# Opening of a two-block kernel: square sums on TensorE, the last shift piece in halves, the step unit two tiles ahead of the x unit, most constants loaded behind the weights

## The reference, cut to what matters

```python
def rmsnorm(x, w, eps=NORM_EPS):
    y = x32 * lax.rsqrt(jnp.mean(x32 * x32, axis=-1, keepdims=True) + eps)
    return y.astype(x.dtype) * w
...
mod = (jax.nn.silu(c) @ w_ada[i] + b_ada[i])[:, None, :]
shift_m, scale_m, gate_m, shift_f, scale_f, gate_f = jnp.split(mod, N_MOD, axis=-1)
h = rmsnorm(x, norm_mix_w[i]) * (1.0 + scale_m) + shift_m
...
proj = h @ w_in     # columns in units; the first are dt (32 columns) and x (256 at a time)
```

## Time and profile before

| | |
|---|---|
| median of 3 runs | 1687.32 us (1686.8 to 1692.4) |
| the profiled execution | 1685.57 us, of which the span of its instructions is 1683.7 us |
| TensorE busy in the span | 1633.9 us (97%) |
| VectorE, ScalarE, GpSimd busy | 881.4, 681.0, 818.2 us |

### The profile page before, as it was taken

One profiled execution on the slowest core, in us unless ns is written; L12 is line 12 of the kernel. 1 busy time (PEld: TensorE's weight loads), 2 busy tenths in 40 slices (PEclk: granted clock), 3 DMA queues, 4 the chain that ended last, 5 costly groups with the idle time before them and its releaser, 6 DMA issues.

```text
span 1683.7 us, 21913 instructions
## 1 busy us (share of the span) xinstructions
PE 1633.9 (97%) x8026; PEld 1362.7 (81%) x8026; DVE 881.4 (52%) x1222; ACT 681.0 (40%) x1103; POOL 818.2 (49%) x670
## 2 busy tenths in 40 slices
PE   6998999999999999999999999999999999999997
PEld 5776888888878788888888889788878888888886
DVE  7556554556585445644336533886456654023324
ACT  3554444445233323532123323445655543234431
POOL 1473655636465545455544454432356354444443
PEclk7999999999999999999999999999999999999999
DMA  8221222122235535344555541221112242232221
GB/s 322 76 75 50 76 76 80 72 76 101 75 103 197 186 139 200 99 164 159 181 198 183 193 163 66 76 100 51 51 51 101 92 147 90 86 124 100 82 91 66
DMA packets 36825, 194.40 MB, mean 115 GB/s; under 512 B 4080, under 2 KB 6384, under 8 KB 21488
## 3 DMA queue, kind: packets, MB, share of 16 engines
q1 hardware_dynamic: 25200, 151.06, 25.0%
q10 hardware_dynamic: 11520, 41.95, 7.4%
HBM read 190.90 MB, written 2.10 MB: 115 GB/s over the span
## 4 chain that ended last, share of the span: by engine, by line
PE 82%; DVE 10%; ACT 4%; issue 2%; POOL 1%; DMA 0%; DVEq 0%; ACTq 0%; SPq 0%; POOLq 0%
PE main L906 61%; PE main L902 6%; PE main L899 3%; PE auxD L1217 1%; DVE tmp L2019 1%; PE main L1006 1%; ACT w_hi L1441 1%; DVE tmp L2584 1%; PE auxD L1282 1%; DVE ysum L2289 1%; POOL w_lo L726 1%; PE auxC L1210 1%; PE auxB L1204 1%; DVE ada_first L2187 0%; PE auxB L1256 0%
## 5 line engine op out<-in xcount | busy, mean ns | idle before, releaser
L726 POOL TENSOR_TENSOR w_lo<-raw,w_hi 128x512 fp32r<-128x512 f32 x521 | 696.2, 1367 | 698.8 <-ACT w_hi L1441 695.0
L906 PE MATMUL main<-h_hi,w_hi 128*128 128x512 f32 (+1 forms) x1016 | 399.8, 394 | 1.4 <-DVEq L2086 1.4
L906 PE MATMUL main<-h_hi,w_lo 128*128 128x512 f32 (+1 forms) x1016 | 396.6, 390 | 0.0
L906 PE MATMUL main<-h_lo,w_hi 128*128 128x512 f32 (+1 forms) x1016 | 396.5, 390 | 0.0
L1441 ACT ACTIVATE w_hi<-raw 128x1024 fp32r<-128x1024 f32 (+2 forms) x267 | 257.8, 1013 | 234.3 <-PE main L906 174.0
L906 PEld LDWEIGHTS main<-h_hi,w_hi 128*128 128x128 f32 (+1 forms) x1016 | 190.9, 188 | 42.1 <-issue 2.6
L906 PEld LDWEIGHTS main<-h_hi,w_lo 128*128 128x128 f32 (+1 forms) x1016 | 190.6, 188 | 40.7
L906 PEld LDWEIGHTS main<-h_lo,w_hi 128*128 128x128 f32 (+1 forms) x1016 | 190.9, 188 | 39.5
L2162 DVE SCALAR_TENSOR_TENSOR tmp<-main,par,tmp 128x511 f32<-128x511 f32 x88 | 65.9, 749 | 161.8 <-ACT tmp L1555 160.0
L2187 DVE SCALAR_TENSOR_TENSOR ada_acc<-ada_raw,cs,ada_acc 128x1024 f32<-128x1024 f32 x70 | 106.9, 1528 | 33.3 <-DMA ada_raw<-w_ada 23.8
L2019 DVE SCALAR_TENSOR_TENSOR tmp<-main,half,tmp 128x511 f32<-128x511 f32 (+2 forms) x96 | 71.8, 748 | 36.5 <-ACT tmp L1464 34.0
(11 more groups left out here) (528 smaller groups left out, 2857.9 us busy)
## 6 DMA issues: line engine op xcount, KB each, us to landing
raw<-stream SPq DMA_DIRECT2D x118, 1024.0 KB, 4.8
ada_raw<-w_ada ACTq DMA_DIRECT2D x80, 512.0 KB, 4.4
ada_first<-w_ada SPq DMA_DIRECT2D x16, 512.0 KB, 10.0
raw<-stream SPq DMA_DIRECT2D x8, 768.0 KB, 4.2
raw<-stream SPq DMA_DIRECT2D x8, 640.0 KB, 3.9
x<-x_in SPq DMA_DIRECT2D x4, 512.0 KB, 6.7
x<-x_in SPq DMA_DIRECT2D x1, 2048.0 KB, 9.4
out<-x SPq DMA_DIRECT2D x16, 128.0 KB, 1.8
```

The source lines that it names most:

```text
L726: nc.gpsimd.tensor_tensor(lo[:, a:b], raw[:, s, a:b], hi[:, a:b], ALU.subtract).then_inc(lo_done, 1)
L906: ins = nc.tensor.matmul(bank[0:n, :], w[:, k, col:col + n], a[:, ka_, :], start=start, stop=stop)
```

## The change

- The constants are reordered; SP loads 268 columns of them first and the other 704 behind units 1 and 2. Two readers of `tri` wait for them (`x_first[0]` at 32).
- DVE's seven adds go. TensorE sums the squares itself: for each k four matmuls with one column of ones, 32 in all, into one accumulating bank. Of the leading identity matmuls 8 of 16 are left. The squares rotate through four slots of `tmp`.
- DVE takes the reciprocal behind the sixth scale piece (k = 5), forms the scale behind the second shift piece, and makes the first two products between shift pieces. The last shift piece is accumulated in two halves, and each half of the shift is summed and biased by itself.
- TensorE runs 6 identity matmuls behind the spread, and 24, in groups of four that wait for the landing of shift pieces 2 to 7, between the two sums.
- ACT copies the `seg` tiles behind the reciprocal, and splits unit 1 in two parts behind the second and third tile of `h_hi` instead of ahead of the first; unit 2 moves from behind the third tile to behind the sixth.
- TensorE's products run in ten steps: in step k the step unit's tile k, and the x unit's tile k - 2.

The diff of the SP program, `first_units`, and the `first_` functions of ACT and DVE:

```diff
-            sp.dma_start(con[:, :], consts_in).then_inc(par_in, 16)
+            sp.dma_start(con[:, 0:FIRST_CONSTS], consts_in[:, 0:FIRST_CONSTS]).then_inc(par_in, 16)
...
+            sp.wait_ge(x_first[0], 16)
+            sp.dma_start(con[:, FIRST_CONSTS:N_CONST], consts_in[:, FIRST_CONSTS:N_CONST]).then_inc(x_first[0], 16)
...
 
             def first_units():
 
-                pair = []
+                first = []
                 for n in range(2):
                     u = units[n]
                     wh, wl = (w.rearrange("p (k c) -> p k c", k=KD) for w in weights(u))
                     rows = min(P, u.cols)
-                    pair += [(u.job0 + t, wh[:, :, P * t:P * t + rows], wl[:, :, P * t:P * t + rows], rows) for t in range(u.n_tiles)]
+                    first.append((u, [(u.job0 + t, wh[:, :, P * t:P * t + rows], wl[:, :, P * t:P * t + rows], rows)
+                                      for t in range(u.n_tiles)]))
 
                 def idle(n):
                     for _ in range(n):
                         nc.tensor.matmul(main[3][:, 0:P], ident, ident, start=True, stop=True)
 
-                idle(16)
+                idle(8)
                 bank, full = take(("norm0", 0), 0)
-                pe.wait_ge(add_first, KD - 1)
-                for c in range(TC):
-                    ins = nc.tensor.matmul(bank[:, chunk(c)], rstd[:, chunk(c)], ones, start=True, stop=True)
-                ins.then_inc(full, 1)
+                for k in range(KD):
+                    pe.wait_ge(norm_sq, k + 1)
+                    for c in range(TC):
+                        ins = nc.tensor.matmul(bank[:, P * c:P * c + 1], first_slot(k)[:, chunk(c)], ones[:, 0:1],
+                                               start=(k == 0 and c == 0), stop=(k == KD - 1 and c == TC - 1))
+                    ins.then_inc(add_first if k < KD - 1 else full, 1)
                 bank, full = take(("norm0", 0), 1)
                 pe.wait_ge(inv_first, 1)
                 for c in range(TC):
                     ins = nc.tensor.matmul(bank[:, chunk(c)], r_col[:, c:c + 1].to_broadcast([P, P]), ident, start=True, stop=True)
                 ins.then_inc(full, 1)
+                idle(6)
                 ada_sum(1, 0)
-                idle(20)
+                for k in range(2, KD):
+                    pe.wait_ge(first_in[k], 32)
+                    idle(4)
                 ada_sum(0, 1)
-                idle(4)
-                for k in range(KD):
+                idle(1)
+
+                def products(u, tiles, k):
+                    end = (k + 1) * u.cols
                     pe.wait_ge(norm_hi, k + 1)
-                    pe.wait_ge(hi_done, high_parts(units[1], (k + 1) * units[1].cols))
-                    for j, wh, wl, rows in pair:
+                    pe.wait_ge(hi_done, high_parts(u, end))
+                    for j, wh, wl, rows in tiles:
                         nc.tensor.matmul(main[j][0:rows, :], wh[:, k, :], h_hi[:, k, :], start=(k == 0), stop=False)
-                    pe.wait_ge(lo_done, low_pieces(units[1], k))
-                    for j, wh, wl, rows in pair:
+                    pe.wait_ge(lo_done, low_pieces(u, k))
+                    for j, wh, wl, rows in tiles:
                         nc.tensor.matmul(main[j][0:rows, :], wl[:, k, :], h_hi[:, k, :], start=False, stop=False)
                     pe.wait_ge(norm_lo, k + 1)
-                    for j, wh, wl, rows in pair:
+                    for j, wh, wl, rows in tiles:
                         ins = nc.tensor.matmul(main[j][0:rows, :], wh[:, k, :], h_lo[:, k, :], start=False, stop=(k == KD - 1))
                         if k == KD - 1:
                             ins.then_inc(main_full[j], 1)
+
+                for step in range(KD + 2):
+                    if step < KD:
+                        products(*first[0], step)
+                    if step >= 2:
+                        products(*first[1], step - 2)
 
             def ada_sum(s, n):
                 if s > 1:
                     for b in range(2):
                         bank, full = take(("ada_sum", s), b)
-                        pe.wait_ge(ada_ready, s + 1)
+                        pe.wait_ge(ada_ready, s + 2)
                         for t in range(4):
                             ins = nc.tensor.transpose(bank[:, chunk(t)], ada_acc[:, chunk(4 * b + t)], ident)
                         ins.then_inc(full, 1)
                     return
-                bank, full = take(("ada_sum", s), 0)
-                pe.wait_ge(ada_ready, 2 - s)
                 acc = ada_first[:, KD * s, :]
-                for t in range(KD):
-                    ins = nc.tensor.matmul(bank[:, t:t + 1], acc[:, chunk(t)], ones[:, 0:1], start=True, stop=True)
-                ins.then_inc(full, 1)
+                for part_ in range(1 if s else 2):
+                    bank, full = take(("ada_sum", s), part_)
+                    pe.wait_ge(ada_ready, 1 if s else 2 + part_)
+                    for t in range(KD) if s else range(4 * part_, 4 * part_ + 4):
+                        ins = nc.tensor.matmul(bank[:, t:t + 1], acc[:, chunk(t)], ones[:, 0:1], start=True, stop=True)
+                    ins.then_inc(full, 1)
...
                 run_act(weight_both, weight_both, ACT.Sqrt, bias=pc("eps2"))
                 for k in range(KD):
                     act.wait_ge(x_first[k // 2], 16)
-                    if k >= 3:
-                        act.wait_ge(add_first, k - 2)
-                    run_act(tmp[:, k % 2, :] if k else rstd[:, :], x[:, k, :], ACT.Square).then_inc(norm_sq, 1)
+                    if k >= 4:
+                        act.wait_ge(add_first, k - 3)
+                    run_act(first_slot(k), x[:, k, :], ACT.Square).then_inc(norm_sq, 1)
                 bank, free = full(("norm0", 0), 0)
                 link(run_act(root, bank[:, :].rearrange("p (c t) -> p c t", c=TC)[:, :, 0], ACT.Sqrt, bias=NORM_EPS_OF[0],
                              scale=1.0 / D_MODEL))
                 act.sem_inc(free, 1)
                 act.sem_inc(norm_rt, 1)
                 split_hi(units[0])
+                act.wait_ge(inv_first, 1)
                 for c in range(TC):
                     ins = run_act(seg_rhs[c][2 * HEADS:P, :, :], over64(cc("slot_of")[2 * HEADS:P, :], P), ACT.Copy)
                 ins.then_inc(seg_set, 1)
-                split_hi(units[1])
                 for k in range(KD):
                     act.wait_ge(norm_tmp, k + 1)
+                    act.wait_ge(mod_ready, 2 if k < 4 else 3)
                     run_act(h_hi[:, k, :], first_slot(k), ACT.Identity, bias=mod_at(0)[:, k:k + 1]).then_inc(norm_hi, 1)
-                    if k == 2:
+                    if k in (1, 2):
+                        split_part(units[1], k - 1)
+                    if k == 5:
                         split_hi(units[2])
...
                     link(tt(to, to, tmp[:, k % 2, :], ALU.add))
                     dve.sem_inc(norm_add, 1)
 
+            def first_product(k):
+                if k == 0:
+                    full(("norm0", 0), 1)
+                b, _ = bank_use["norm0", 0][1]
+                if k >= 4:
+                    dve.wait_ge(norm_lo, k - 3)
+                ins = stt(first_slot(k), x[:, k, :], mul[:, 0, k:k + 1], aux[b][:, :], ALU.mult, ALU.mult)
+                if k == KD - 1:
+                    link(ins)
+                    dve.sem_inc(aux_free[b], 1)
+                    dve.sem_inc(norm_tmp, 1)
+                else:
+                    ins.then_inc(norm_tmp, 1)
+
+            def first_low(k):
+                dve.wait_ge(norm_hi, k + 1)
+                dve.wait_ge(norm_tmp, k + 1)
+                stt(h_lo[:, k, :], first_slot(k), mod_at(0)[:, k:k + 1], h_hi[:, k, :],
+                    ALU.add, ALU.subtract).then_inc(norm_lo, 1)
+
+            def first_shift(part_):
+                bank, free = full(("ada_sum", 0), part_)
+                ks = slice(4 * part_, 4 * part_ + 4)
+                link(tt(mod_at(0)[:, ks], bank[:, ks], pc("b_ada", 4 * part_, 4 * part_ + 4), ALU.add))
+                dve.sem_inc(free, 1)
+                dve.sem_inc(mod_ready, 1)
+
             def first_sums():
 
-                for k in range(1, KD):
-                    dve.wait_ge(norm_sq, k + 1)
-                    link(tt(rstd[:, :], rstd[:, :], tmp[:, k % 2, :], ALU.add))
-                    dve.sem_inc(add_first, 1)
-                for s in (1, 0):
-                    for k in range(KD):
-                        dve.wait_ge(first_in[k], 16 if s else 32)
-                        add_piece(s, k, ada_first[:, KD * s + k, :])
-                        if s and k == 1:
-                            dve.wait_ge(norm_rt, 1)
-                            nc.vector.reciprocal(r_col, root).then_inc(inv_first, 1)
+                for k in range(KD):
+                    dve.wait_ge(first_in[k], 16)
+                    add_piece(1, k, ada_first[:, KD + k, :])
+                    if k == 5:
```

(40 more changed lines are left out.)

17 lines of the change are left out of this document (13 added, 4 removed).

## The result

The changed kernel takes 1691.66 us (median of 20 runs) against 1687.28 for the kernel before (20 runs on the same chips). The ratio is 1.0023, 95% interval [1.0014, 1.0032], which is 3.9 us more (2.4 to 5.4). One of the changed kernel's 20 runs took 2745.6 us at a mean granted clock of 0.55; the ratio goes by the other 19. The forecast was no change within 0.3%, at 1690.0.

The account below looks back on a forecast made before the run. TensorE is busy 97%; the first 56.4 us were VectorE's queue to 35.2, a 4.4 us hand-over and 16.8 us of TensorE. Last product 59.6 less 56.4 gives +3.2: 1688.8, or 1690.5 on the median; forecast 1690, range 1684 to 1694.

Parts of the forecast that it names:

- +3.2 us for unit 2: End of the opening: last product at 59.6 instead of 56.4, so unit 2 and the whole 3.2 us later.
- the signs that I had named: VectorE waits of 1.25 and 2.7, squares at 0.43, first product at 40.5 to 41, gaps, unit 2 at 59 to 60.
- the starved steps: Product steps 0 to 2 on TensorE: steps 0 and 1 hold 3 products each, step 2 waits for `h_lo` 2.
- Constants: 0.85: Head of SP's queue: 352 KB moved back are worth 0.85 us; first scale piece lands at 12.3.
- Squares: 13.7 us: TensorE's 32 one-column matmuls: 0.43 each at the lower clock, ending at 20.8; VectorE waits 1.25 for the reciprocal.
- rival B: Clock up through the squares: they end by 14.1, VectorE waits 0.7 at the scale's sum; 0 change, 1687.3; chance 0.20.
- The scale's sum: TensorE behind six identity matmuls: 3.58 us at the lower clock, ending at 29.2; VectorE waits 2.7 us from 26.5.
- The shift: four sums at the upper clock, 1.1: Behind the last half piece at 38.5: four sums take 1.1, bias 0.25, shift at 39.85, 2.0 us late.
- Rival C: Products start at the lower clock: 2.65 us lost, 0.85 for four sums; +6.7, 1694 on the median; chance 0.18.
- The low parts: VectorE from shift to `h_lo` 2: 5.0 us, ready at 44.9, two low parts at 0.95; 14.7 us of products left.
- D: No wait at the scale's sum, low parts keep up: last product at 53.3, -3.1, 1684.2 on the median; chance 0.10.
- One to one behind unit 2: TensorE goes on without rest behind the opening, so a shift of unit 2's start counts one to one.

Follow-up runs that it names:

- the opening before: The kernel before plus three groups of identity matmuls in TensorE's waits between 98 and 112 us; opening unchanged, unit 2 at 59.04; ratio 1.0001 to the kernel before.
- the second run: The changed kernel itself, unchanged, traced and timed again on another chip; ratio 1.0022 to the kernel before.
- the joint runs: Four variants of the changed kernel with the x unit's products beside the step unit's for the same k; ratios to the kernel before 1.0010, 1.0016, 1.0000, 0.9995.
- joint products: Changed kernel with the ten steps undone: nine products a k, unit 1 split ahead of `h_hi`; ratio 1.0010 to the kernel before.
- constants in front: Changed kernel with one load of all constants at the head again; ratio 1.0023 to the kernel before.
- scale late: Changed kernel with VectorE's scale bias behind the seventh shift piece and the products behind the shift's pieces; ratio 1.0015 to the kernel before.
- the fills: Changed kernel plus identity matmuls (5, 4, 6, 12, 9) in five TensorE waits between 98 and 167 us; ratio 1.0024 to the kernel before.
- the scale one piece later: Changed kernel with VectorE forming the scale behind its third shift piece instead of the second; ratio 1.0013 to the kernel before.
- the run with joint products and identity matmuls: Changed kernel with the ten steps undone and twelve more identity matmuls ahead of the shift's sums; ratio 1.0016 to the kernel before.
- the identity matmuls alone: Changed kernel with twelve more identity matmuls ahead of the shift's sums; ratio 1.0020 to the kernel before.
- the one with all: Scale late plus joint products, eight identity matmuls ahead of the shift's sums, three between its parts, three behind instead of one; ratio 1.0000 to the kernel before.
- the run with all and fills: The one with all, plus identity matmuls (5, 4, 6) in three TensorE waits between 98 and 112 us; ratio 0.9995 to the kernel before.

## Why the prediction was right, step by step

**The verdict and the sum.** No change within 0.3% was forecast, with +3.2 us for unit 2; the ratio's 3.9 us (2.4 to 5.4) and the trace's 3.6 agree. But the 3.6 are made of other sizes than the 3.2. The shift was to come 2.0 us later and came 1.2 later; from there to unit 2 I had 1.2 us more than before, and it was 2.4. Two misses of a microsecond cancelled, which is luck. That 3.6 meets 3.9 is in part luck too: set against the other trace of the opening before (unit 2 at 59.04), it would be 1.0. Of the signs that I had named, the first product at 40.78, the starved steps and unit 2 at 60.05 came; the wait at the reciprocal (none, for 1.25), that at the scale's bias (1.06, for 2.7) and squares at 0.43 from first to last did not, in this trace.

**Constants: 0.85.** The size held (0.8, by one run against ten). The level didn't: the first scale piece starts at 13.1 in the mean, where I had it landed at 12.3.

**Squares: 13.7 us, ending at 20.8, VectorE waiting 1.25.** The forecast and rival B are both true, each in some executions. The eleven traces with squares on TensorE have them end between 18.1 and 22.3. In four they ran at 0.43 all through, 13.65 to 13.81 us, and VectorE waited 1.19 to 1.74 at the reciprocal: the forecast's case. In seven the clock was up at their start and fell during them, and VectorE didn't wait: half of rival B, for its clock was not up to their end in any trace. The eight identity matmuls ahead of them took 0.45 us each (3.98 to 7.55 in the second run), not my 0.38, which I had read as the lower pace from a row of sixteen that sped up on its way (5 records in its first 1.08 us, 10 in its last 1.16). The Trainium skill's rule that I had set against the forecast (TensorE: Matmul & The Clock Gate, the section on the HAM clock gate: "the default state is throttled, and activity releases the throttle") agrees with the traces on the rise ahead of the squares in those seven. It does not in the other four, three of which show TensorE without a gap from 4 to 21 us at the lower pace, nor on the fall while the squares go on; there the measurement decides.

**The scale's sum: at the lower clock, VectorE waiting 2.7.** The step failed: the clock rose at 25.0, during the six identity matmuls behind the spread, the sum took 1.84 instead of 3.58, and VectorE waited 1.06 (0.8 to 1.6 in the other traces with this order), nearer to rival B's 0.7. That is 1.6 us less than I had. The mechanism held, and moving the bias took the wait away.

**The shift: four sums at the upper clock, 1.1.** They took 1.84, since the clock had fallen at 35.3. Rival C had the danger, with the price of 0.85 for the four sums; the forecast had not. With the 1.6 of the step above it gives the shift 0.9 us earlier than forecast.

**The low parts: `h_lo` 2 5.0 us behind the bias.** Mis-sized by 1.1: it was 6.1 behind the bias's end. The trace has an idle of 0.73 ahead of the second low part, put down to ScalarE's `h_hi` and in no term of mine, and 1.22 and 1.11 for two low parts that I had at 0.95. What stands behind the 0.73 wasn't tried; the joint runs have it too (0.72 to 0.73), so it isn't ScalarE's split of unit 1 between the tiles. `h_lo` 2 was ready at 45.1 (forecast 44.9) and unit 2 began at 60.05, 14.9 behind it (14.7). The starved steps are shown by the runs with the clock up: 18.7 to 18.8 with joint products against 21.1 with the steps, 2.3 us.

**Rivals.** C, products at the lower clock, came true as a fact and mostly not in its price: the starved steps hid it, as said. Where the clock was down behind the third low part (constants in front, scale late) it cost 1.8 more, and 2.4 in the opening before; I had 2.65. D fell: VectorE does wait. What no rival had is that the kernel before pays the lower clock too, in some executions: its unit 2 at 56.46 was a good one.

**One to one behind unit 2.** Right to 0.1 us in twelve of fourteen traces as far as 131 to 138 us; in two another 3.1 us were lost to the clock. Over the whole kernel it isn't shown: from unit 2 to the end of the span it is 1627.2 us before and 1627.9 in the changed kernel, but 1624.7 with joint products and 1631.0 with the fills. The run with joint products starts unit 2 1.8 us later than the changed kernel and ends 1.4 earlier. Where these microseconds go behind 138 us wasn't followed up.

**What stays open.** The ratios' intervals are some 4 us wide, so single terms of 1 us (the scale's wait, the adds, the constants) are told by stretches of the traces, not by the times. The 3.9 us, a mean over executions, can't be split further; only the joint products together with the late scale and the added identity matmuls brought them back to zero.

## What to carry to other kernels

Work taken off an engine is worth only the time in which its next input is already there: 5.72 us of adds gave some 1.5, by one trace. A wait newly put into an in-order queue is paid by all that stands behind it, and an early consumer (the scale's products) ahead of a late producer (the shift's pieces) delays the chain that ends last. Where TensorE starves, look at what the clock will be when dense work starts, and take more than one trace of the opening before you price it to a microsecond.

## What the runs showed of the hardware

**The level at the start is read from the pace, not from PEclk.** Two rows of 8 to 10 us, during the squares, of the changed kernel's second run and of the run with the scale one piece later:

```profile
8.00:10.00 2.00, 2.00 (x19) 1.00 1.00 370
...
8.00:10.00 2.00, 2.00 (x11) 1.00 1.00 391
```

Both print a granted clock of 1.00, but 19 records against 11 are the upper and the lower pace (0.22 and 0.43 a matmul). The column stands at 1.00 until the first change is recorded. The same code is at either level there, from execution to execution.

**One-column matmuls without a gap did not hold the clock.** In the changed kernel's second run TensorE had no gap from 3.98 to 18.1 us, and the clock fell at 11.4 amid the squares. In the run with joint products the same matmuls, again without a gap, stayed at the lower pace to 21.3. The squares of these two:

```profile
7.55 10.55 PE L1108 MATMUL auxC<-con,tmp 128*128 128x1 f32 x64
...
7.62 13.65 PE L1108 MATMUL auxC<-con,tmp 128*128 128x1 f32 x64
```

In the run with joint products and identity matmuls the clock fell between the two sets of one-column sums, which pauses of 0.53 and 0.56 us preceded. In the run with the identity matmuls alone and in the one with all it stayed up over the same sums.

**Two engines slow each other down.** While GpSimd split weights, a piece on VectorE took 2.34 instead of 1.28 us (joint products), its halves 1.65 instead of 0.83 each, and most low parts 1.1 to 1.8 instead of 0.74. GpSimd's four pieces took 6.82 us beside them, and 4.97 in the run with all and fills, where VectorE was idle for most of that time. VectorE's products, which read one operand from PSUM (`auxD`), kept their 0.73 to 0.75 beside the same split in the changed kernel.
